# One block of a mixed transformer on one core: attention pairs weigh, score, then turn; the first norm on VectorE and ScalarE; half an output product moved in one stage

## What is computed

```python
def rms_norm(x, g):
    return x * lax.rsqrt(jnp.mean(x * x, axis=-1, keepdims=True) + EPS) * g

# first_block: moba, cross, relu
h = rms_norm(x, pre_mix_g);  y = concat(spatial_gating, moba_attention, conformer_conv)(h @ w_in) @ w_out
x = x + rms_norm(y, post_mix_g)
x = x + rms_norm(memory_cross_attention(rms_norm(x, pre_x_g), rms_norm(mem, mem_g), ...), post_x_g)
x = x + rms_norm(jnp.square(jax.nn.relu(h @ w_ff1)) @ w_ff2, post_ffn_g)
# second_block, twice: glu, attention (diff, then near), glu
h = h + 0.5 * rms_norm(swiglu(rms_norm(h, g0)), g1)
h = h + rms_norm(attention(rms_norm(h, g2)), g3)
h = h + 0.5 * rms_norm(swiglu(rms_norm(h, g4)), g5)
```

## Time and profile before

| | |
|---|---|
| median of 3 runs | 1386.82 us |
| the profiled execution | 1386.52 us, of it 1384.8 us from first to last instruction |
| TensorE, matmuls | 1372.4 us (99%) |
| TensorE, weight loads beside them | 1154.2 us (83%) |
| VectorE | 890.1 us (64%) |
| ScalarE | 742.5 us (54%) |
| GpSimd | 150.8 us (11%) |
| read from memory | 253.14 MB, 184 GB/s over the span |

### The profile page before, as it was taken

The page is one execution under the profiler, slowest core; times in us unless marked ns, Lnnn a source line. Parts: engine busy times, 40 slices in busy tenths (PEclk is TensorE's granted clock), DMA queues, the critical chain, the costliest instruction groups (busy, mean ns, idle before and its releaser), DMA issues.

```text
span 1384.8 us, 18120 instructions
## 1 busy us (share of the span) xinstructions
PE 1372.4 (99%) x7261; PEld 1154.2 (83%) x7261; DVE 890.1 (64%) x1037; ACT 742.5 (54%) x984; POOL 150.8 (11%) x251
## 2 busy tenths in 40 slices
PE   8999999999999999999999999999999999999998
PEld 7988888888888888878788888888888877888886
DVE  5986657665567666665876665665666656676663
ACT  6647556444455444555764444554444667554443
POOL 1000102111011111110211110121170100000000
PEclk9999999999999999999999999999999999999999
DMA  9854435756548656554357656485655644365550
GB/s 313 304 171 152 136 139 184 229 196 202 186 154 249 191 200 198 172 191 143 129 163 226 200 193 192 167 238 192 195 197 166 206 138 137 122 228 186 194 168 31
DMA packets 121362, 255.38 MB, mean 184 GB/s; under 512 B 6393, under 2 KB 32829, under 8 KB 121278
## 3 DMA queue, kind: packets, MB, share of 16 engines
q1 hardware_dynamic: 117036, 250.99, 55.4%
q0 software_dynamic: 4096, 3.15, 0.9%
q10 hardware_dynamic: 146, 0.07, 0.0%
HBM read 253.14 MB, written 1.05 MB: 184 GB/s over the span
## 4 chain that ended last, share of the span: by engine, by line
PE 97%; ACT 1%; issue 1%; DVE 0%; DMA 0%; POOL 0%; DVEq 0%; ACTq 0%; POOLq 0%
PE ps L1656 21%; PE ps L1364 18%; PE ps L1366 18%; PE ps L1365 18%; PE ps L1657 10%; PE ps L1352 1%; PE ps L1354 1%; PE ps L1353 1%; PE ps L1377 1%; PE ps L1387 1%; PE ps L1424 1%; PE ps L1469 1%; PE ps L1631 1%; PE ps L1397 1%; PE ps L1691 1%
## 5 line engine op out<-in xcount | busy, mean ns | idle before, releaser
L972 DVE TENSOR_TENSOR w_lo<-raw,w_hi 128x2048 fp32r<-128x2048 f32 x225 | 516.4, 2300 | 278.9 <-ACT w_hi L679 277.2
L679 ACT CAST w_hi<-raw 128x2048 fp32r<-128x2048 f32 x225 | 428.2, 1910 | 213.9 <-PE ps L1366 137.4
L1656 PE MATMUL ps<-hT,w_hi 128*128 128x512 f32 x1216 | 429.2, 397 | 0.0
L1657 PE MATMUL ps<-hT,w_lo 128*128 128x256 f32 x1216 | 340.7, 280 | 0.0
L1656 PEld LDWEIGHTS ps<-hT,w_hi 128*128 128x128 f32 x1216 | 228.3, 188 | 55.4 <-issue 0.2
L1364 PE MATMUL ps<-w_hi,yT_hi 128*128 128x512 f32 x640 | 252.8, 395 | 0.7 <-DVE yT_lo L1232 0.7
L1366 PE MATMUL ps<-w_hi,yT_lo 128*128 128x512 f32 x640 | 249.6, 390 | 0.0
L1365 PE MATMUL ps<-w_lo,yT_hi 128*128 128x512 f32 x640 | 249.3, 390 | 0.0
L1657 PEld LDWEIGHTS ps<-hT,w_lo 128*128 128x128 f32 x1216 | 229.5, 189 | 0.8
L1364 PE MATMUL ps<-w_hi,hT 128*128 128x512 f32 (+1 forms) x496 | 193.8, 391 | 0.0
L1366 PE MATMUL ps<-w_hi,hT 128*128 128x512 f32 (+1 forms) x496 | 188.6, 380 | 0.0
(11 more groups left out here) (196 smaller groups left out, 1253.5 us busy)
## 6 DMA issues: line engine op xcount, KB each, us to landing
raw<-ffn_wd SPq DMA_DIRECT2D x44, 1024.0 KB, 5.3
raw<-ffn_wg SPq DMA_DIRECT2D x40, 1024.0 KB, 5.6
raw<-ffn_wu SPq DMA_DIRECT2D x40, 1024.0 KB, 5.4
raw<-w_ff SPq DMA_DIRECT2D x32, 1024.0 KB, 5.9
raw<-diff_w_in SPq DMA_DIRECT2D x12, 1024.0 KB, 5.5
raw<-na_w_in SPq DMA_DIRECT2D x12, 1024.0 KB, 5.3
raw<-w_in SPq DMA_DIRECT2D x10, 1024.0 KB, 6.7
raw<-w_xkv SPq DMA_DIRECT2D x8, 1024.0 KB, 11.3
```

Source lines behind the costliest of these rows:

```text
L679: act.copy(hi_part(c), raw[:, c % NRAW, :]).then_inc(hi_done, 1)
L972: dve.tensor_tensor(lo_part(c), raw[:, c % NRAW, :], hi_part(c), ALU.subtract).then_inc(lo_done, 1)
L1656: pe.matmul(o, wh[:, i, cols], h_both[:, k, :, :], start=first and i == 0, stop=False)
L1657: ins = pe.matmul(o[:, 0:256], wl[:, i, cols], hT[0][:, k, :], start=False, stop=last and i == 3)
```

## The change

It has three parts. In `attention_pairs` S(s) moves in front of P(2s-2). In the plan of diff `o2.1` is split into halves, and half a moves in front of `o3.0`. The first norm of x is computed without GpSimd: VectorE sums the squares of the first half of row tile 0 (`tensor_tensor_reduce`, which adds EPS), ScalarE squares the second half and takes the root of the sum (`Sqrt`, with the other half's sum as its bias), and VectorE takes the reciprocal; for row tile 1 ScalarE squares both halves and VectorE only adds EPS. A root of a constant is put in front, so that ScalarE has the table of the root. The memory's norm stays with GpSimd; the counts of its semaphores shift by two.

```diff
--- before.py
+++ after.py
@@ attention_pairs
-        words += [f"W{s - 2}"] * out + [f"P{2 * s - 2}"] * last + [f"S{s}"] * now + [parts[0]] + [f"P{2 * s - 1}"] * last
+        words += [f"W{s - 2}"] * out + [f"S{s}"] * now + [f"P{2 * s - 2}"] * last + [parts[0]] + [f"P{2 * s - 1}"] * last
@@ PLAN, diff
-             "h l o2.0b o3.0 post0 gain0 o2.1 o3.1a sq0 turna0 o3.1b post2 turnb0"),
+             "h l o2.0b o2.1a o3.0 post0 gain0 o2.1b o3.1a sq0 turna0 o3.1b post2 turnb0"),
@@ GpSimd
             pool.wait_ge(const_set, 1)
-            for n in range(2):
-                for t in range(TT):
-                    pre_root(n, t)
+            for t in range(TT):
+                pre_root(1, t)
@@ ScalarE
-            def squares(n, src, src_ready):
+            def first_squares(t):
+                act.wait_ge(x_in[t], 16)
+                for b in range(2) if t else (1,):
+                    to = 2 * CH + t * D + 512 * b
+                    act.activation(big[:, to:to + 512], x[:, t, 512 * b:512 * b + 512], ACT.Square, scale=1.0 / 32,
+                                   accum_out=ssq[:, t, b:b + 1]).then_inc(first_sq, 1)
+                act.wait_ge(first_sq, 2 * t + 1)
+                act.wait_ge(first_sum, t + 1)
+                act.activation(rstd[:, t:t + 1], ssq[:, t, 1:2], ACT.Sqrt, bias=end_sum[:, t:t + 1]).then_inc(first_root, 1)
...
-            squares(0, x, lambda t, b: act.wait_ge(x_in[t], 16))
+            act.wait_ge(const_set, 2)
+
+            act.activation(lam[:, 6:7], eps_col[:, 0:1], ACT.Sqrt)
+            for t in range(TT):
+                first_squares(t)
             for t in range(TT):
                 turned_hi(0, t, hT)
                 split_first(t)
             split()
             split()
-            squares(1, mem_rows, lambda t, b: act.wait_ge(mem_in, 16))
+            mem_squares()
@@ VectorE
+            def first_sums(t):
+                if t == 0:
+                    dve.wait_ge(x_in[0], 16)
+                    dve.tensor_tensor_reduce(big[:, 2 * CH:2 * CH + 512], x[:, 0, 0:512], x[:, 0, 0:512], 1.0 / D, EPS,
+                                             ALU.mult, ALU.add, end_sum[:, 0:1]).then_inc(first_sum, 1)
+                else:
+                    dve.wait_ge(first_sq, 2)
+                    dve.tensor_scalar(end_sum[:, 1:2], ssq[:, 1, 0:1], EPS, None, ALU.add).then_inc(first_sum, 1)
+
             def first_rows(n, src, t):
                 k = TT * n + t
-                dve.wait_ge(r_pre, k + 1)
+                if n == 0:
+                    dve.wait_ge(first_root, t + 1)
+                    link(dve.reciprocal(rstd[:, k:k + 1], rstd[:, k:k + 1]))
+                else:
+                    dve.wait_ge(r_pre, t + 1)
...
             for t in range(TT):
+                first_sums(t)
                 first_rows(0, x, t)
```

More of the change, by code:

```diff
@@ L360, in build @@
         end_sum_set, end_root_set = sem("end_sum_set"), sem("end_root_set")
+        first_sq, first_sum, first_root, first_scale = (
+            sem(n) for n in ("first_squares", "first_sum_set", "first_root_set", "first_scale_set"))
         s_ready, m_ready, e_ready, p_ready, t_ready, pt_ready, o_ready, o_hi, o_lo = (
@@ L613, in pre_root @@
                 k = TT * n + t
-                row_root(k, sq_pre, 2 * (k + 1), r_pre)
+                row_root(k, sq_pre, 2 * (k + 1 - TT), r_pre)
                 if n >= 2 and STAGES[n - 1] in GROUPS:
-                    pool.wait_ge(r_pre, k + 1)
+                    pool.wait_ge(r_pre, k + 1 - TT)
                     pool.tensor_scalar(q_scale[:, t:t + 1], rstd[:, k:k + 1], -ATT[STAGES[n - 1]]["scale"], None,
@@ L696, in square, with mem_squares @@
                 dumped[b] = (done, count)
-            def squares(n, src, src_ready):
+            def first_squares(t):
[7 more added lines that the diff above has]
+                act.activation(rstd[:, t:t + 1], ssq[:, t, 1:2], ACT.Sqrt, bias=end_sum[:, t:t + 1]).then_inc(first_root, 1)
+            def mem_squares():
+                act.wait_ge(mem_in, 16)
                 for t in range(TT):
                     for b in range(2):
[L702 to L705, removed]
+                        to = t * D + 512 * b
+                        act.activation(big[:, to:to + 512], mem_rows[:, t, 512 * b:512 * b + 512], ACT.Square, scale=1.0 / 32,
+                                       accum_out=ssq[:, TT + t, b:b + 1]).then_inc(sq_pre, 1)
             def turned_hi(n, t, dst, halves=(0, 1)):
@@ L735, in norm_word @@
                         act.wait_ge(x_new, 2 * (TT * j + t) + b + 1)
-                        count = 2 * (TT * n + t) + b + 1
+                        count = 2 * (TT * (n - 1) + t) + b + 1
                         square(x[:, t, 512 * b:512 * b + 512], b, ssq[:, TT * n + t, b:b + 1], sq_pre, count)
@@ L868, in rows_word @@
                     act.wait_ge((half_used, used)[t], AT_CHUNK[kind, letter + "bd"[nb], 0] + 1)
-                    act.wait_ge(r_pre, k + 1)
+                    act.wait_ge(r_pre, k + 1 - TT)
                     if g == 0:
@@ L901, in hidden_word @@
                         if b == 0:
-                            act.wait_ge(r_pre, TT * (word.at + 1) + t + 1)
+                            act.wait_ge(r_pre, TT * word.at + t + 1)
                         k = TT * (word.at + 1) + t
@@ L1255, in late_scales @@
             def late_scales(kind, word, t, k):
-                dve.wait_ge(r_pre, k + 1)
+                dve.wait_ge(r_pre, k + 1 - TT)
                 r = rstd[:, k:k + 1]
@@ L1280, in hidden_word @@
                     for i in range(TT):
-                        dve.wait_ge(r_pre, TT * (word.at + 1) + i + 1)
+                        dve.wait_ge(r_pre, TT * word.at + i + 1)
                         dve.tensor_scalar(scale_in[:, i * P:i * P + P], ident, 0.0, rstd[:, k + i:k + i + 1],
```

## The result

| | before | after |
|---|---|---|
| median | 1386.74 us (6 runs) | 1395.24 us (6 runs, 1394.26 to 1395.84) |
| ratio | | 1.0054, 95% interval 1.0043 to 1.0064 |
| profiled execution | 1386.52 us, span 1384.8 | 1395.84 us, span 1394.1 |
| TensorE, matmuls | 1372.4 us | 1375.3 us |

The change makes the kernel slower by 8.5 us. The executions of most kernels here fall into two groups 1 to 2 us apart (of 75 of the kernel before, 39 lie between 1386.48 and 1386.93 and 36 between 1387.94 and 1388.96), so medians jump with the mix, and where a tenth counts I compare lower group with lower group and upper with upper.

A forecast was written before the change was run, and what follows sets the result against it. TensorE, busy for 99% of the span, was taken to bound the kernel. Near +5.8, moba +2.0, head -0.6 and diff +0.4 sum to +7.6 us, from the median 1386.82 to 1394.4 us; range 1389.8 to 1396.9.

The forecast's parts named there:

- Near, +5.8: Seven near steps: the second turning waits for ScalarE's copy of the first, 0.83 us more per step, 5.8 in all.
- 0.14 us of handover: Pairs' steps: time from the end of ScalarE's copy to the next turning, 0.14 us, read from one moba row.
- W before S: Pairs' steps: weighing directly before scores, taken to last 1.02 us, as weighing before a turning does.
- bounds on it (1.4 us either way): Weighing before scores might be 0.17 us shorter or longer in 6 near and 2 moba steps: 1.4 us either way.
- Moba, +2.0: Moba steps 1 to 3: same wait for the copy, +0.73 us in steps 2 and 3, +0.53 in step 1.
- Diff, +0.4: End of diff: 0.90 us stall before o3.0 gone, 0.91 back before turna, 0.45 lost at the next stage.
- what stood behind it: Diff: the path o3.0, square, root, add, gain, turna loses cover, 18 matmuls (4.1 us) down to 12 (2.8 us).
- Head, -0.6: First norm of x: rows of tile 0 start 0.83 us sooner, the first product 0.6 us sooner.
- the work behind is TensorE's own, so the gain stays: After the head: TensorE's work has no waits on DMA until the end, so the 0.6 us gain is kept.
- The first rival: Pairs' steps: the copy doesn't hold the second turning, ten steps each win the 0.17 us changeover; 1383.1 us, chance 0.05.
- The third: Diff keeps its gain: the path from o3.0 to turna shortens, -0.9 instead of +0.4 us; 1393.2 us, chance 0.15.
- The second rival: Pairs cost little: no changeover before scores and an early copy, some 0.3 us a step; 1388.5 us, chance 0.07.

The follow-up runs named there:

- e7: Pairs ordered turn, weigh, score, turn, with ScalarE's first copy before its copy of the weighed values, against the kernel before: 1387.21 us, ratio 0.9993.
- e2: Only the first norm of x changed, against the kernel before; pairs and diff as before: 1386.72 us, ratio 0.9997.
- e3: Only the half output product in diff moved (o2.1a before o3.0), against the kernel before: 1386.94 us, ratio 0.9996.

## Why the prediction was right, and where it was not

The predicted time was 1394.4, measured 1395.24; the sum was +7.6, measured +8.5. Most of the difference is the mix of groups in the six runs on each side. Over all ten runs of the changed kernel and those of before, it is +7.8 from lower group to lower group (middles 1394.4 and 1386.6) and +7.3 from upper to upper (1395.8 and 1388.5). Sign, mechanism and three of the four terms came out.

- **Near, +5.8: measured 5.78.** The 0.14 us of handover taken from one row of moba is 0.14 in near too. W before S costs what W before P did, the nearer row. The bounds on it (1.4 us either way) were not needed. The seven steps are not alike, though: steps 2 to 7 take 0.81 us more each (0.83 expected), step 1 takes 0.96, since S now stands behind a product there and pays the 0.09 us that e7 shows. That these two even out is luck.
- **Moba, +2.0: measured 2.00.** Step 1 holds a wait of the same size as steps 2 and 3 (1.20 to 1.22 us between the turnings in all three), as assumed.
- **Diff, +0.4: measured 0.32 to 0.37.** The stall in front of o3.0 was exchanged for one in front of turna and one before glu1. As idle time they are 0.65 and 0.23 us, but busy ends are modelled; by starts, turna comes 0.81 us late (0.91 expected: the last matmul starts at 701.64, 1.04 instead of 0.23 before it) and glu1's product 0.48 (0.45 expected: 0.83 behind turnb's start, before 0.35). The step "what stood behind it" was right: the path o3.0 to turna had half a microsecond of slack and the move took more.
- **Head, -0.6: measured -0.1 (lower groups, e2) and -0.7 (upper groups).** In the first profiled execution the rows came at 6.17 (6.15 predicted) and the first product at 11.71 (11.8 predicted), 0.70 us sooner. The +1.17 us at moba's first scores between the two profiled executions is no price of the change: the one of before had the full clock from 12.13 us, that of after from 16.12. Two steps failed in part. The term was worked out from one landing of the gain row (2.3 us); where it lands at 2.7 the start gains 0.2 to 0.4. And "the work behind is TensorE's own, so the gain stays" does not hold at the lower clock, where a sooner start is worth 0.58 of itself. I had read the pace of 0.215 us per turning off and not asked when it ends; that moment differs between executions and moves the kernel by up to 2 us (moba's first scores at 103.02 to 105.20 with the old head), more than the whole term.
- **The first rival** (the changeover decides) had the right effect, of nearly the right size, in an order that loses more to the copy: 0.15 us a step can be had, by e7, where the copy stays covered. **The third** (diff keeps its gain) is refuted by e3. The second rival had its premise (the copy begins early) refuted by the same 0.70 us in each step. The prices given for the second and third rivals are 0.1 to 0.2 us too high by their own terms (1386.82 + 3 - 1.5 = 1388.3, and 1394.4 - 1.3 = 1393.1); no chance hangs on that.

## What to carry to other kernels

When two users of one buffer are put next to each other, the distance between them is the hand-over and back, not their own length: read it off any place where the second already waits (here one row of 0.2 us), and price the reorder with it. A stall that a moved piece of work fills is won only if the path behind has slack: count the cover that the piece gave where it stood. And TensorE at the start of a program may still run at its lower clock, until a moment that differs from one execution to the next: look where the first full-clock record begins in each trace, and compare early executions with early ones, or the mix is taken for the effect of an edit at the head. Work brought forward at the lower clock is worth about half of its lead (0.58 here). The cost of a changeover can lie in the matmul ahead of it: measure a step from the last start before it.

## What was not expected of the hardware

The same first 24 matmuls of the first product take 3.0 us in some executions and 4.4 to 5.1 in others, with the same head of the program. The full clock is granted at 10.7 to 12.1 us in the ones and at 15.5 to 17.4 us in the others; this splits the times into two groups 1 to 2 us apart and is larger than several of the edits tested. A turning costs 0.11 us more in front of matmuls that write 64 columns and 0.17 in front of ones that read 64 rows, and a product's matmul 0.09 us more in front of either; but matmuls of the first kind take the same 1.02 us whether the second kind or a turning follows.
